# Products of zeros ahead of five known waits of TensorE

## The reference

```python
o_a = gated_head_norm(gated_delta_rule_chunked(q_a, k_a, v_a, g_dec, beta), ...)
o_b = gated_head_norm(hgrn2_chunked(q, k, v, log_f), ...)
h = h + rms_norm(concat(o_a, o_b) @ w_out, post_mix_norm)
h = h + rms_norm(square(relu(rms_norm(h, pre_mlp_norm) @ w_mlp_up)) @ w_mlp_down, ...)
h = h + rms_norm(p @ w_ple_proj, ple_norm) * sigmoid(h @ w_ple_gate)
h = concat(meta, h);  xv, bg, cg, ga, gg = split(rms_norm(h) @ w_in_2)
y_sc = bg * conv3(cg * xv);  y_cf = silu(layer_norm(conv31(ga * sigmoid(gg)) + b))
h = h + concat(rms_norm(y_sc), rms_norm(y_cf)) @ w_out_2
h = h + peer_layer(rms_norm(h), ...);  return rms_norm(h)[:, 16:]
```

## Time and profile before

| | us |
|---|---|
| median of 3 runs (lowest, highest) | 1452.34 (1451.54, 1452.35) |
| profiled execution, its own time | 1450.62 |
| its span, first to last instruction | 1448.8 |
| PE busy | 1357.2 (94%) |
| DVE busy, ACT busy | 886.8, 783.4 |
| mean granted clock of PE | 0.974 |

### The profile page before, as it was taken

One profiled execution on the slowest core, in us unless ns is written; L12 is line 12 of the kernel. 1 busy time (PEld: TensorE's weight loads), 2 busy tenths in 40 slices (PEclk: granted clock), 3 DMA queues, 4 the chain that ended last, 5 costly groups with the idle time before them and its releaser, 6 DMA issues.

```text
span 1448.8 us, 26132 instructions
## 1 busy us (share of the span) xinstructions
PE 1357.2 (94%) x8934; PEld 1235.7 (85%) x8934; DVE 886.8 (61%) x1667; ACT 783.4 (54%) x1377; POOL 412.0 (28%) x239
## 2 busy tenths in 40 slices
PE   4999958999998976899999999999999999999997
PEld 4998946999976975799999999999998888888885
DVE  3677355666567885479994255656635555555554
ACT  4645314444445733447777676676655555555553
POOL 0100301000001671007988766666650000000001
PEclk9999978999999997899999999999999999999998
DMA  6533004555544442245555544444455555555553
GB/s 233 175 118 115 30 0 155 188 188 188 190 159 146 146 146 73 102 160 170 179 188 187 176 145 135 144 146 137 141 172 186 184 185 186 187 188 188 188 184 106
DMA packets 62008, 225.16 MB, mean 155 GB/s; under 512 B 7136, under 2 KB 7520, under 8 KB 61552
## 3 DMA queue, kind: packets, MB, share of 16 engines
q1 hardware_dynamic: 59904, 217.61, 44.5%
q10 hardware_dynamic: 2032, 6.60, 1.2%
HBM read 223.13 MB, written 1.05 MB: 155 GB/s over the span
## 4 chain that ended last, share of the span: by engine, by line
PE 88%; DVE 5%; POOL 2%; ACT 2%; issue 2%; DMA 1%; ACTq 0%; POOLq 0%; DVEq 0%
PE bank L497 76%; PE bank L920 4%; POOL arena L1440 1%; DVE arena L1842 1%; PE bank L520 1%; PE bank L570 1%; PE bank L691 1%; PE bank L477 1%; ACT arena L973 1%; PE bank L701 1%; PE bank L699 1%; DMA arena<-in_meta 1%; ACT w_hi L1003 1%; PE bank L713 1%; PE bank L873 0%
## 5 line engine op out<-in xcount | busy, mean ns | idle before, releaser
L1003 ACT ACTIVATE w_hi<-ring 128x1024 fp32r<-128x1024 f32 x414 | 438.7, 1060 | 516.6 <-PE bank L497 342.2
L1513 DVE TENSOR_TENSOR w_lo<-ring,w_hi 128x1024 fp32r<-128x1024 f32 x274 | 338.3, 1235 | 311.9 <-ACT w_hi L1003 305.5
L497 PE MATMUL bank<-hT_hi,w_hi 128*128 128x256 f32 (+2 forms) x1728 | 432.4, 288 | 3.6 <-DVE hT_lo L1505 1.4
L497 PE MATMUL bank<-hT_lo,w_hi 128*128 128x256 f32 (+2 forms) x1728 | 424.1, 283 | 0.0
L1467 POOL TENSOR_TENSOR w_lo<-ring,w_hi 128x1024 fp32r<-128x1024 f32 x128 | 310.5, 2428 | 172.9 <-ACT w_hi L1003 172.7
L497 PEld LDWEIGHTS bank<-hT_hi,w_hi 128*128 128x128 f32 x1728 | 328.0, 190 | 7.0 <-issue 2.9
L497 PEld LDWEIGHTS bank<-hT_lo,w_hi 128*128 128x128 f32 x1728 | 328.9, 190 | 0.1
L497 PE MATMUL bank<-hT_hi,w_lo 128*128 128x256 f32 (+2 forms) x1728 | 240.7, 282 | 5.7 <-POOL w_lo L1449 5.7
L497 PEld LDWEIGHTS bank<-hT_hi,w_lo 128*128 128x128 f32 x1728 | 221.2, 190 | 6.1 <-POOL w_lo L1449 6.1
L497 PE MATMUL bank<-w_hi,wgt_hi 128*128 128x512 f32 x504 | 200.0, 397 | 0.0
L497 PE MATMUL bank<-w_hi,wgt_lo 128*128 128x512 f32 x504 | 199.8, 396 | 0.0
(11 more groups left out here) (318 smaller groups left out, 1598.7 us busy)
## 6 DMA issues: line engine op xcount, KB each, us to landing
ring<-in_stream SPq DMA_DIRECT2D x414, 512.0 KB, 3.2
arena<-in_rows ACTq DMA_DIRECT2D x1, 1536.0 KB, 17.4
consts<-in_consts ACTq DMA_DIRECT2D x1, 1152.0 KB, 12.5
h<-in_x ACTq DMA_DIRECT2D x1, 1024.0 KB, 7.4
arena<-in_keys ACTq DMA_DIRECT2D x1, 1024.0 KB, 4.7
arena<-in_rows ACTq DMA_DIRECT2D x1, 512.0 KB, 3.6
out_h<-arena SPq DMA_DIRECT2D x2, 256.0 KB, 2.1
out_h<-arena ACTq DMA_DIRECT2D x2, 256.0 KB, 2.5
```

The source lines that it names most:

```text
L497: mm = nc.tensor.matmul(o, a, b, start=first and not low_part and xp is x[0], stop=last and low_part)
L1003: nc.scalar.activation(w_hi[:, g % S, :], ring[:, g % R, :], ACT.Copy).then_inc(hi_done, 1)
L1513: nc.vector.tensor_tensor(w_lo[:, g % S, :], ring[:, g % R, :], w_hi[:, g % S, :].bitcast(F32), ALU.subtract).then_inc(lo_done, 1)
```

## The change

A function `idle_products(b, n)` issues n products of zeros, 128x512 in bf16, into bank b, each a sum of its own. It is called at five places of PE's stream: 45 into bank 6 ahead of `transposes(1)`, 16 into bank 0 ahead of `open_sums` and `transposes(2)`, 14 into bank 7 ahead of `transposes(4)`, 50 into bank 7 ahead of the column sums, 16 into bank 7 ahead of `transposes(5)`. No other engine's stream changes.

```diff
+            def idle_products(b, n):
+
+                for _ in range(n):
+                    nc.tensor.matmul(bank[b][:, :], zb, zb.unsqueeze(1).to_broadcast([P, HALF // P, P]),
+                                     start=True, stop=True)
...
             heads(5, lambda hd: decayT[:, 2 * hd + 1, :], hcol(vnew[:, 1, :])).then_inc(oa_full, 1)
+            pe.wait_ge(zeroed, 1)
+            idle_products(6, 45)
             transposes(1)
...
+            idle_products(0, 16)
             open_sums()
             transposes(2)
...
             pe.wait_ge(gsig_out, 4)
+            pe.wait_ge(weighted_done, 12)
+            idle_products(7, 14)
             transposes(4)
             pe.wait_ge(meta_in_hT, 1)
...
             for b in range(NH):
                 taken_in2(16 + b)
+            idle_products(7, 50)
             pe.wait_ge(cf_done, 2)
             column_sums(mean, cfacc, (0, 1))
...
+            idle_products(7, 16)
             transposes(5)
```

More of the change, by code:

```diff
@@ L464, in hT_block @@
                 pe.wait_ge(tr_lo, KD * n + k + 1)
+            zb = zeros[:, :].bitcast(BF16)
+            def idle_products(b, n):
+                for _ in range(n):
+                    nc.tensor.matmul(bank[b][:, :], zb, zb.unsqueeze(1).to_broadcast([P, HALF // P, P]),
+                                     start=True, stop=True)
             def transposes(n):
```

## The result

The changed kernel takes 1455.9 us (10 runs, 1454.2 to 1458.36) against 1452.34 us (10 runs, 1450.1 to 1454.3): ratio 1.0026, 95% interval 1.0016 to 1.0036, so 2 to 5 us slower. It was measured twice more, with 1.0039 (1.0026 to 1.0053) and 1.0035 (1.0022 to 1.0047).

A forecast was written before the change was run, and what follows sets the result against it. The prediction took PE, busy for 94% of the span, and its waits to set the time. Terms +11.0 - 0.3 - 1.0 - 0.3 - 0.8 = +8.6 us on 1452.34 gave 1461 us, range 1458.3 to 1464.5.

The forecast's parts named there:

- D: 13.5 us pause ahead of the column sums: 50 products cost 13.4 us, warm work behind saves 2.4, so +11.0 us.
- D starts when its pause ends: The 50 products wait for DVE's line 1917, so they start at 552.1 and delay everything behind them on PE's queue.
- A: 13.2 us pause ahead of the first output projection: 45 products leave 3.5 us idle; taken -0.3 us, between +1.1 and -1.1.
- B: 5.3 us pause to 241.42, ahead of `transposes(2)`: 16 products leave 1.8 us idle; taken -1.0 us, between 0 and -1.6.
- C: 4.6 us pause to 464.38, ahead of `transposes(4)`: 14 products run until 464.0; gain 0.3 us, at least 0.
- E: 5.4 us pause to 596.91, ahead of `transposes(5)`: 16 products leave 1.9 us; taken -0.8 us, between 0 and -1.1.
- sixth: Pause of 4.51 us ahead of the fifth tile of the second output projection; the prediction had no term for it.
- Four fills that hold nothing: Rival: idle time left in A, B and E costs the clock again, only D counts: 1463.3 us, chance 0.21.
- D hidden: Rival: PE starts the 50 products while DVE still works, saving 2.4 us: 1445.8 us, or 1447.5; chance 0.05.
- Zeros don't count as work: Rival: the clock stays at half through D, 21.3 us of products, the others gain nothing: 1473.7 us, chance 0.04.
- The page on transposes: If transposes never get full clock, gains through earlier transposes vanish and the change costs about 10 us, not 8.6.

The follow-up runs named there:

- e3: The change with D's 50 products moved ahead of the wait that ends the pause, into bank 5: ratio 0.9963 against the kernel before.
- e10: The change with 25 products instead of 50 at the same place of D: 1451.72 against 1451.14 us for the kernel before, ratio 1.0007.
- e7: As e3, with D's moved fill lengthened from 50 to 60 products: ratio 0.9948 against the kernel before.
- e1: The kernel before with only D's 50 products, the four other fills left out: 1461.62 against 1450.38 us, ratio 1.0076.
- e2: The change without D's 50 products, keeping the fills A, B, C and E: ratio 0.9968 against the kernel before.
- e12: The same kernel as e2 measured again, beside the change on one chip: 1446.15 us, ratio 0.9968 against the kernel before.
- e8: The kernel before with only 8 products, into bank 4 ahead of the last wait for DVE's weights: ratio 0.9986.
- e6: The change with fills of 59, 23, 15, 60 and 24 products, D moved, plus 19 in the sixth pause: 1442.21 against 1451.13 us, ratio 0.9936.

## Why the prediction was right in its main step and too large in its sum

*The step that failed* is the sum's account of what the clock gives back. It put the end, the half clock behind the short pause near 1433 us, at nothing without a reason: it was gone in all three profiles of the change, worth 1.5 us. And it took the four fills at -2.4 us, where they measured -3.3. The mechanism of D, and that of the fills, were right.

*D starts when its pause ends.* Right. The row of the first product names DVE's line 1932 as its releaser; moving the 50 products (e3) takes the price away, and halving them (e10) takes half of it. The terms were right as well: 13.4 us of products against 13.3, 2.4 us of warm work behind against 2.3 (e7), +11.0 against +10.8 in stretch D and +11.0 in time (e1).

*The fills.* Right in how they work, mis-sized. Means over the profiles of the table, four without fills against the eight with the change's four numbers:

| term | forecast, taken | its limit | measured |
|---|---|---|---|
| A | -0.3 | -1.1 | 22.46 to 22.04: -0.4 |
| B | -1.0 | -1.6 | 21.27 to 19.76: -1.5 |
| C | -0.3 | -0.3 | 17.30 to 16.87: -0.4 |
| E | -0.8 | -1.1 | 21.51 to 20.58: -0.9 |

Together -3.3 instead of -2.4. B was the worst: I held 1.8 idle us for little better than even odds, since 1.95 us had cost the clock near the end, and seven of eight kept it. My steps for B don't add up as written: 1.1 us to the low pass and 0.2 in it make 1.3, or 1.7 with the 0.4 of ACT. Measured in the change's first profile are 1.3 to the low pass and 0.35 in it (1.10 us, not 1.45), together the limit of 1.6, so that this number came out by luck. For A "seldom" was right: with 45 products, which leave 3.5 us, two profiles of eight kept the clock through. But the -0.3 doesn't follow from seldom -1.1 and otherwise up to +1.1; it came out because a clock that fell cost less than that, -0.5 to +0.4 us against the mean without fills.

*What the sum left out.* The end. I used the half clock behind the last short pause as evidence and never as a term. Without fills all three profiles that have this pause unfilled lost 1.5 us there; with the change's four fills seven of eight didn't, though nothing was changed within 800 us. On average this gives -1.3. With the fills' -3.3 it makes the -4.6 us that e2 and e12 measured. Why the fills move it isn't settled, and with this few profiles part of it may be chance. e8 shows that the pause does cost the clock in the kernel before and what that is worth; that the fills avoid it by the moment at which the pause comes is argued, not shown, and e6 and e10 have fills and lost it all the same.

*The sum.* Three measurements of the change gave +3.8, +5.7 and +5.0, mean +4.8. The traces give nearly the same once the start stretch is left out, which no kernel touches and which took 193.4 to 198.3 us: the mean of the change's three profiles against that of the two of before is +5.5. Term by term, as forecast and as these five profiles have it:

| term | forecast | measured |
|---|---|---|
| D | +11.0 | +10.75 |
| sixth | 0 | -0.4 |
| A, B, C, E | -2.4 | -3.3 |
| end | 0 | -1.5 |
| sum | +8.6 | +5.5 |

So 3.1 us of the miss are found, half of them at the end; the 0.7 us from +5.5 to +4.8 are within the intervals. The parts measured alone, +11.0 - 4.6 = +6.4, agree with this within theirs. The first measurement, +3.8, lies lowest of the three; beside it the kernel before had the highest of its medians, 1452.34 against 1450.4 to 1451.2. My range was too narrow at its low end, since that end took D at 10.1 and the fills near their best, but no term for the end or the sixth pause and nothing for the scatter of the start.

*The rivals.* Four fills that hold nothing: wrong (e2). D hidden: wrong; placed so that it is hidden, D belongs to kernels that take -5.4 and -7.5 us (e3, e7). Zeros don't count as work: wrong. Behind 5.2 us of products alone (550.91 to 556.1) the clock rose, and it held through 13.1 us of them in e7.

*The page on transposes.* The Trainium skill, TensorE: Matmul & The Clock Gate, section Part 4: PE-mode transpose, has the full clock not engage for transpose-mode. Here eight transposes took 1.09 us at a granted clock of 1.00 behind a fill, and sixteen 3.67 us at 0.50 without one, so the measurement decides for these. The rows call them MATMUL, and don't show whether they use the mode that the page speaks of.

## What to carry to other kernels

Ahead of a fill of idle time ask which wait ends the pause, and put the fill in front of that wait, into a buffer that some earlier wait frees: behind it each product costs its full length, here 11 us against -2.3. Fill up to half a microsecond of the end, since 1.8 to 3.5 us left over cost the clock in part of the profiles, and 0.6 us or less in none. A term for the clock wants several profiles, and every stretch that one profile shows at half clock belongs in the sum, those that the change doesn't touch too.

## What the runs showed of the hardware

Products of zeros in bf16 kept the clock up: through 60 of them, 13.12 us, it stayed at 1.00 (e7). From start to start they took 0.216 us at full and 0.427 us at half clock, 128x512. At D they started at 550.91 and the clock rose at 556.1, 5.2 us later; real work before started at 552.30 and had it at 557.3. In all runs together the mean granted clock and the span give the time at half clock: 79 to 81 us of 1451 before (the profiled execution, at 0.974 x 1448.8, had 75), 45 to 49 with the change, 18 with everything filled (2 x (1 - clock) x span, mean over the runs of each). The start, a stretch of code that no edit touches, took 193.42 us in e12 with 3.4 us of half clock in it and 198.30 in e3 with 13.6; 10.2 us more at half speed can cost up to 5.1 us, and the two differ by 4.9.
